# Retrieval in a decoder trunk: 80 sums of key pairs for each head in place of 256

## The chip, the cores and the metric

The kernel runs on one core of a Trainium2 chip. A core has TensorE (PE, matrix products), VectorE (DVE), ScalarE (ACT), GpSimd (POOL) and SyncE (SP, which issues transfers), each with a queue of its own that it works off in order; they wait for one another by semaphores. The metric is the time of one execution on the device in microseconds (us), the median of several runs.

## The reference, cut to what matters

One layer of a decoder trunk is computed for 512 prompt tokens and 64 sample tokens. The part that matters here is the retrieval of single-neuron experts: each token has 8 heads, and each head takes the 16 best of 128 keys on two sides, adds every pair of the two lists, and keeps the 16 best of the 256 sums. From the place of such a sum follow the two keys, and from them the expert's number.

```python
q = (xt @ w_q).astype(jnp.float32).reshape(n, PEER_HEADS, 2, PEER_QDIM // 2)
s = jnp.einsum('nhsd,hskd->nhsk', q, subkeys.astype(jnp.float32))
v_top, i_top = lax.top_k(s, PEER_TOPK)                  # 16 of 128, sorted
cand = (v_top[:, :, 0, :, None] + v_top[:, :, 1, None, :]).reshape(n, PEER_HEADS, PEER_TOPK * PEER_TOPK)
cand_idx = (i_top[:, :, 0, :, None] * PEER_KEYS + i_top[:, :, 1, None, :]).reshape(n, PEER_HEADS, PEER_TOPK * PEER_TOPK)
vals, cpos = lax.top_k(cand, PEER_TOPK)                 # 16 of 256
eidx = jnp.take_along_axis(cand_idx, cpos, axis=-1)
gate = jax.nn.softmax(vals, axis=-1)
```

Both lists are sorted downwards. The sum of entry a of the one and entry b of the other has at least (a + 1)(b + 1) - 1 sums that are no smaller, so it can be among the 16 best only where (a + 1)(b + 1) is at most 16.

## The kernel before

The program is a row of stages: projections, the two mixers, `mix_stage`, then `retrieve_stage`, `gate_matrix_stage`, `experts_stage` and `ple_stage`. Each of these ends with a barrier of all engines. The change touches `retrieve_stage` alone, which lies at 874 to 1182 us of the profiled span.

It does two things side by side. The tokens are taken in five tiles (`TILES`; 128, 128, 128, 64 and 128 rows), with these steps for tile t:

- PE makes the scores of 16 lists of 128 keys (line 1993) and ACT copies them to `scores` (line 1862), one of two buffers.
- DVE runs `select(t)`: for each of the 16 lists the best 8 (`max`, line 1892), their places (`max_index`, 1895), a copy with these 8 struck out (`match_replace`, 1896), the next 8 and their places (1899, 1902). Then for each head the 256 sums of the pairs (line 1909, into the buffer that held the scores), and over these the same five passes (1914 to 1925). Lines 1926 to 1931 subtract the largest value and make two numbers a and b from each place by a shift and a mask. Lines 1936 to 1940 fetch the two keys: a comparison with 0 to 15, a product, a sum, for each side.
- ACT takes exponentials (line 1847); DVE makes the gates (`gates(t)`, lines 1946 to 1952), which stands behind `select(t + 1)` in its queue; PE transposes the picks (line 1982) and ACT copies them to `idxT` (line 1852).

Beside it 50 units of expert products run, for which SP loads a block of weights, ACT makes its high half (line 1831), POOL its low half (line 1879), PE 24 products (line 1571, `dense_products`) and ACT an activation (line 1840). `SELECT_TURNS` says how many units PE does in each tile before and after the transposes of an earlier tile: 4 + 8, 4 + 8, 4 + 4, 4 + 4, 4 + 6. The transposes of tile t stand behind the first four units of tile t + 2, those of the fourth tile behind the last unit; the fifth tile's picks are used as they are. PE's scores of the next tile stand behind all units of the present one. `v.go` sends an instruction without a wait behind it, `v(...)` waits until it is done, `v.wait()` until all are.

The order of each engine is written out by hand; nothing is moved by a scheduler.

Of the kernel before, what the change touches and what calls it, by code (L numbers as in the profile page):

```python
# [15 lines left out]
U32 = mybir.dt.uint32  # L16
# [3 lines left out]
P = 128  # L20
# [28 lines left out]
PH = 8  # L49
# [1721 lines left out]


SELECT_TURNS = ((4, 8), (4, 8), (4, 4), (4, 4), (4, 6))
SELECT_UPS = sum(map(sum, SELECT_TURNS))
SELECT_FROM = [sum(map(sum, SELECT_TURNS[:t])) for t in range(TILES)]
ONE_HOT_UPS = TD // 32
SAMPLE_TILE = TILES - 1
EARLY_GROUPS = (SELECT_UPS + ONE_HOT_UPS) // EG
assert EG * EARLY_GROUPS == SELECT_UPS + ONE_HOT_UPS and SELECT_UPS % 2 == 0


def retrieve_stage(nc, k):

    with ExitStack() as ctx:
        sb = lambda n, s, d=F32: ctx.enter_context(nc.sbuf_tensor(n, s, d))
        sem = k.sem
        sk, iota = sb("subkeys_sb", [P, 16, KEYS]), sb("iota16", [P, 16])
        scores, scr = sb("k_scores", [P, 2, 16, KEYS]), sb("k_scr", [P, 16, KEYS])
        v16, i16, i16f = sb("v16", [P, 16, 16]), sb("i16", [P, 16, 16], U32), sb("i16f", [P, 2, 16, 16])
        eq = sb("eq", [P, PH, 16, 16])  # L1790
        vals, cpos, ab = sb("vals", [P, 2, PH, 16]), sb("cpos", [P, PH, 16], U32), sb("ab", [P, 2, PH, 16], U32)
        abf, idx, gsum = sb("abf", [P, 2, PH, 16]), sb("idx", [P, 2, 3, P]), sb("gsum", [P, 2, PH])
        u_raw, u_hi, u_lo = sb("r_u_raw", [P, EG, KD, P]), sb("r_u_hi", [P, 2, KD, P]), sb("r_u_lo", [P, 2, KD, P])

# [7 lines left out]
        up_done, gelu_done, u_hi_made, u_lo_made = (sem(n) for n in ("r_up", "r_gelu", "r_u_hi_made", "r_u_lo_made"))  # L1802
        N = SELECT_UPS
        block = ctx.enter_context(nc.Block())
# [23 lines left out]
        def _(act):  # L1828
# [4 lines left out]
            def group(first, count):  # L1833
                for n in range(first, first + count):
                    e = n % EG
                    act.wait_ge(up_done, n + 1)
                    if n >= EG and e % 2 == 0:

                        act.wait_ge(k.spilled[e // 2], 16 * (n // EG))
                    nc.scalar.activation(gelu[:, e // 2, e % 2], ps[:, 4 + n % 2, 0:TD], ACT.Gelu_apprx_tanh).then_inc(gelu_done, 1)  # L1840
                    if n + 2 < N:
                        u_high(n + 2)
# [14 lines left out]
            for t in range(TILES):  # L1857
# [4 lines left out]
                nc.scalar.activation(scores[0:m, t % 2].rearrange("p (b n) c -> p b (n c)", b=4), ps[0:m, 0:4, :], ACT.Copy).then_inc(scopied, 1)  # L1862
                half, rest = SELECT_TURNS[t]
                group(SELECT_FROM[t], half)
# [16 lines left out]
        @block.vector  # L1881
        def _(dve):
            v = Chain(dve, vch)
            V = nc.vector

            def select(t):

                m, b = PICK_ROWS[t], t % 2
                sc = scores[0:m, b]
                dve.wait_ge(scopied, t + 1)  # L1890
                for u in range(16):
                    v.go(V.max(v16[0:m, u, 0:8], sc[:, u]))
                v.wait()
                for u in range(16):
                    v.go(V.max_index(i16[0:m, u, 0:8], v16[0:m, u, 0:8], sc[:, u]))
                    v.go(V.match_replace(scr[0:m, u], v16[0:m, u, 0:8], sc[:, u], GONE))
                v.wait()
                for u in range(16):
                    v.go(V.max(v16[0:m, u, 8:16], scr[0:m, u]))
                v.wait()  # L1900
                for u in range(16):
                    v.go(V.max_index(i16[0:m, u, 8:16], v16[0:m, u, 8:16], scr[0:m, u]))
                v.wait()
                v.go(V.tensor_copy(i16f[0:m, b].rearrange("p a b -> p (a b)"), i16[0:m].rearrange("p a b -> p (a b)")))

                cand = sc.rearrange("p a b -> p (a b)").rearrange("p (h c) -> p h c", h=PH)
                left = scr[0:m].rearrange("p a b -> p (a b)").rearrange("p (h c) -> p h c", h=PH)
                for h in range(PH):
                    v.go(V.tensor_tensor(cand[:, h].rearrange("p (a b) -> p a b", a=16),
                                         v16[0:m, 2 * h].unsqueeze(2).to_broadcast([m, 16, 16]),  # L1910
                                         v16[0:m, 2 * h + 1].unsqueeze(1).to_broadcast([m, 16, 16]), ALU.add))
                v.wait()
                for h in range(PH):
                    v.go(V.max(vals[0:m, b, h, 0:8], cand[:, h]))
                v.wait()
                for h in range(PH):
                    v.go(V.max_index(cpos[0:m, h, 0:8], vals[0:m, b, h, 0:8], cand[:, h]))
                    v.go(V.match_replace(left[:, h], vals[0:m, b, h, 0:8], cand[:, h], GONE))
                v.wait()
                V.memset(gsum[0:1, 0, 0:1], 0.0).then_inc(s_used, 1)  # L1920
                for h in range(PH):
                    v.go(V.max(vals[0:m, b, h, 8:16], left[:, h]))
                v.wait()
                for h in range(PH):
                    v.go(V.max_index(cpos[0:m, h, 8:16], vals[0:m, b, h, 8:16], left[:, h]))
                v(V.tensor_copy(gsum[0:m, 0], vals[0:m, b, :, 0]))
                V.tensor_tensor(vals[0:m, b], vals[0:m, b], gsum[0:m, 0].unsqueeze(2).to_broadcast([m, PH, 16]),
                                ALU.subtract).then_inc(eready, 1)
                v.go(V.tensor_scalar(ab[0:m, 0], cpos[0:m], 4, None, ALU.logical_shift_right))
                v(V.tensor_scalar(ab[0:m, 1], cpos[0:m], 15, None, ALU.bitwise_and))  # L1930
                v(V.tensor_copy(abf[0:m].rearrange("p a h c -> p (a h c)"), ab[0:m].rearrange("p a h c -> p (a h c)")))
                if t >= 2:
                    dve.wait_ge(trd, t - 1)
                e3 = eq[0:m].rearrange("p h c a -> p (h c) a")
                for s in range(2):
                    v(V.tensor_tensor(e3, abf[0:m, s].rearrange("p h c -> p (h c)").unsqueeze(2).to_broadcast([m, P, 16]),
                                      iota[0:m].unsqueeze(1).to_broadcast([m, P, 16]), ALU.is_equal))
                    fs = i16f[0:m, b].rearrange("p (h s) a -> p h s a", s=2)[:, :, s]
                    v(V.tensor_tensor(eq[0:m], eq[0:m], fs.unsqueeze(2).to_broadcast([m, PH, 16, 16]), ALU.mult))
                    v(V.tensor_reduce(idx[0:m, b, s], e3, AX.X, ALU.add))  # L1940

            def gates(t):

                m, b = PICK_ROWS[t], t % 2
                dve.wait_ge(ed, t + 1)
                v(V.tensor_reduce(gsum[0:m, 0], vals[0:m, b], AX.X, ALU.add))
                v(V.reciprocal(gsum[0:m, 1], gsum[0:m, 0]))
                if t == SAMPLE_TILE:
                    V.scalar_tensor_tensor(out=k.s_idx[0:m], in0=idx[0:m, b, 0], scalar=float(KEYS), in1=idx[0:m, b, 1],
                                           op0=ALU.mult, op1=ALU.add)  # L1950
                out = k.s_gate[0:m] if t == SAMPLE_TILE else idx[0:m, b, 2]
                V.tensor_tensor(out.rearrange("p (h c) -> p h c", h=PH), vals[0:m, b],
                                gsum[0:m, 1].unsqueeze(2).to_broadcast([m, PH, 16]),
                                ALU.mult).then_inc(tk, 1)

            dve.wait_ge(ld, 32)
            for t in range(TILES):
                select(t)
                if t >= 1:
                    gates(t - 1)  # L1960
            gates(TILES - 1)

        @block.tensor
        def _(pe):
# [21 lines left out]
            for t in range(TILES):  # L1986
# [8 lines left out]
                mm.then_inc(sd, 1)  # L1995
                half, rest = SELECT_TURNS[t]
                group(SELECT_FROM[t], half)
# [10 lines left out]
def gate_matrix_stage(nc, k):  # L2008
# [4 lines left out]
    with ExitStack() as ctx:  # L2013
# [12 lines left out]
        up_done, gelu_done, u_hi_made, u_lo_made = (sem(n) for n in ("gm_up", "gm_gelu", "gm_u_hi_made", "gm_u_lo_made"))  # L2026
        FIRST = SELECT_UPS
        UPS = ONE_HOT_UPS // 2
# [9 lines left out]
        def _(sp):  # L2038
# [25 lines left out]
            for q in range(2):  # L2064
                sp.wait_ge(k.spilled[q], 16 * ((SELECT_UPS // 2 - q + 1) // 2))
            for b in range(2):
# [898 lines left out]
```

## Time and profile before

| | us |
|---|---|
| median of 3 runs | 2481.58 (2476.61 to 2482.66) |
| profiled execution | 2492.35 |
| its span, first to last instruction | 2490.7 |
| PE busy in the span | 2196.4 (88%) |
| DVE busy | 1747.6 (70%) |
| ACT busy | 771.1 (31%) |
| POOL busy | 721.2 (29%) |

The shares are means over stages with different limits. What a change inside a stage is worth is read from that stage: which engine waits for which there, and which wait ends last. Times in the rows further down are us from the span's start unless they are marked ns. In the views by time a row gives the start, the length, the engine, line, operation, output <- input, shapes and count, and in brackets how long the engine was idle in front of it and who ended that.

### The profile page before, as it was taken

What the parts mean: (1) busy time and instruction counts of PE and PEld (TensorE: products, weight loads), DVE (VectorE), ACT (ScalarE), POOL (GpSimd) and SP (SyncE); (2) the same over time, 40 slices, a digit from 0 to 9 for tenths busy, and PEclk for the clock granted to TensorE, in tenths of its full rate; (3) what the DMA queues carried; (4) which work ended last, traced back from release to release, by engine and by line L of the source; (5) the groups of instructions that cost most, each with busy time, mean ns of one, the idle gap of its engine ahead of it and who ended that gap; (6) DMA issues with size and microseconds to landing.
All of it is one profiled execution on the core that took longest, in us unless ns stands there. A gap on an engine that the chain in (4) does not pass through costs nothing. (4 is left out here: it accounts for less than half of the span.)

```text
span 2490.7 us, 36671 instructions
## 1 busy us (share of the span) xinstructions
PE 2196.4 (88%) x11589; PEld 1911.2 (77%) x11589; DVE 1747.6 (70%) x3908; ACT 771.1 (31%) x1376; POOL 721.2 (29%) x653
## 2 busy tenths in 40 slices
PE   7885599777698999985899689999999999999979
PEld 5444389544488989974888678888899999999968
DVE  6845300466322089999999689999889898888852
ACT  2021211354322233331454323333323233232331
POOL 0411311201132344441444222222433333333302
PEclk9987799588898999997999899999999999999999
DMA  5204623412421144440766667778888787878721
GB/s 207 19 24 61 206 81 122 122 56 89 153 77 52 50 172 145 133 146 25 256 186 204 201 246 291 291 291 308 305 286 294 274 309 273 303 274 286 254 89 39
DMA packets 194121, 448.24 MB, mean 180 GB/s; under 512 B 26401, under 2 KB 109602, under 8 KB 184610
## 3 DMA queue, kind: packets, MB, share of 16 engines
q1 hardware_dynamic: 140082, 222.74, 27.3%
q0 software_dynamic: 44288, 156.92, 18.8%
q10 hardware_dynamic: 9648, 67.24, 6.8%
q8 instruction: 60, 0.98, 0.2%
q14 instruction: 43, 0.35, 0.0%
HBM read 394.07 MB, written 54.80 MB: 180 GB/s over the span
## 5 line engine op out<-in xcount | busy, mean ns | idle before, releaser
L2591 PE MATMUL e_ps<-w_hi,v_hi 128*128 128x448 f32 x1024 | 379.8, 371 | 25.2 <-DVE w_lo L2485 15.3
L2591 PE MATMUL e_ps<-w_lo,v_hi 128*128 128x448 f32 x1024 | 378.3, 369 | 0.0
L2591 PE MATMUL e_ps<-w_hi,v_lo 128*128 128x448 f32 x1024 | 378.1, 369 | 0.0
L2591 PEld LDWEIGHTS e_ps<-w_hi,v_hi 128*128 128x128 f32 x1024 | 194.1, 190 | 48.9 <-issue 23.5
L2591 PEld LDWEIGHTS e_ps<-w_hi,v_lo 128*128 128x128 f32 x1024 | 194.1, 190 | 18.0
L2591 PEld LDWEIGHTS e_ps<-w_lo,v_hi 128*128 128x128 f32 x1024 | 194.1, 190 | 17.7
L1571 PE MATMUL e_ps<-x_hi,u_hi 128*128 128x448 f32 x512 | 189.5, 370 | 17.9 <-DVE u_lo L2420 17.9
L1571 PE MATMUL e_ps<-x_lo,u_hi 128*128 128x448 f32 x512 | 189.4, 370 | 0.0
L1571 PE MATMUL e_ps<-x_hi,u_lo 128*128 128x448 f32 x512 | 189.2, 370 | 0.0
L2430 DVE TENSOR_TENSOR hT<-hT,e_ps 128x448 f32<-128x448 f32 x256 | 157.5, 615 | 31.6 <-PE e_ps L2591 31.6
L2324 ACT ACTIVATE v_hi<-v_raw 128x512 fp32r<-128x512 f32 x256 | 157.2, 622 | 68.0 <-PE e_ps L2591 62.3
L2424 DVE TENSOR_TENSOR v_lo<-v_raw,v_hi 128x512 fp32r<-128x512 f32 x256 | 174.9, 685 | 0.3
L1879 POOL TENSOR_TENSOR r_u_lo<-r_u_raw,r_u_hi 128x1024 fp32r<-128x1024 f32 x50 | 125.0, 2500 | 167.4 <-ACT r_u_hi L1831 167.4
L2276 POOL DMA_INDIRECT s_rows<-in_v_rows,s_idx x62 | 76.2, 1229 | 296.3 <-DVE s_rows L2451 295.7
L2125 PE MATMUL g_ps<-one_hot 128*128 128x128 f32 x896 | 134.1, 289 | 22.6 <-DVE one_hot L2093 22.6
L2125 PEld LDWEIGHTS g_ps<-one_hot 128*128 128x128 f32 x896 | 126.1, 194 | 32.8 <-DVE one_hot L2093 29.8
L1571 PE MATMUL r_ps<-x_hi,r_u_hi 128*128 128x448 f32 x400 | 148.2, 371 | 1.0 <-POOL r_u_lo L1879 1.0
L1571 PE MATMUL r_ps<-x_hi,r_u_lo 128*128 128x448 f32 x400 | 147.0, 368 | 0.0
L1571 PE MATMUL r_ps<-x_lo,r_u_hi 128*128 128x448 f32 x400 | 147.0, 368 | 0.0
L2093 DVE TENSOR_SCALAR one_hot<-iota,idx_T 128x128 f32<-128x128 f32 x448 | 144.0, 341 | 0.0
L2335 ACT ACTIVATE w_hi<-w_raw 128x448 fp32r<-128x448 f32 x128 | 73.6, 575 | 219.7 <-DVE w_raw L2494 200.6
L2353 ACT ACTIVATE e_act<-e_ps 128x448 f32<-128x448 f32 x64 | 34.8, 545 | 326.7 <-PE e_ps L1571 326.7
(538 smaller groups left out, 5059.5 us busy)
## 6 DMA issues: line engine op xcount, KB each, us to landing
v_raw<-in_v_tab ACTq DMA_DIRECT2D x62, 1024.0 KB, 7.0
u_raw<-in_u_tab SPq DMA_DIRECT2D x64, 512.0 KB, 6.0
gate_scr<-gate_stage SPq DMA_DIRECT2D x14, 2048.0 KB, 9.3
mixT<-gate_scr SPq DMA_DIRECT2D x32, 896.0 KB, 5.9
r_u_raw<-in_u_tab SPq DMA_DIRECT2D x50, 512.0 KB, 3.9
gelu_scr<-mixT SPq DMA_DIRECT2D x32, 448.0 KB, 2.7
acts_and_rows<-gelu_scr SPq DMA_DIRECT2D x16, 896.0 KB, 7.3
m_w_raw<-in_w_mix SPq DMA_DIRECT2D x24, 512.0 KB, 3.5
```

The source lines that it names most:

```text
L1571: mm = pe.matmul(out, as_r(u), as_r(x[:, i, 0:TD]), start=(i == 0 and n == 0), stop=(i == KD - 1 and n == 2))
L1879: nc.gpsimd.tensor_tensor(as_r(u_lo[:, n % 2]), u_raw[:, n % EG], u_hi[:, n % 2], ALU.subtract).then_inc(u_lo_made, 1)
L2093: nc.vector.tensor_scalar(oh2[:, n % 8], iota[:], k.idxT[:, 1, at], k.idxT[:, 2, at], ALU.is_equal, ALU.mult).then_inc(hot, 1)
L2125: mm = nc.tensor.matmul(ps[:, q % 4, KEYS * (n % 4):KEYS * (n % 4) + KEYS], oh1[:, n % 8], oh2[:, n % 8], start=True, stop=True)
L2276: pool.indirect_dma_start(out=ring[j], out_offset=None, in_=k.d[table], in_offset=bass.IndirectOffsetOnAxis(ap=s_idx[:, slot:slot + 1], ax ...
L2324: nc.scalar.activation(as_r(v_hi[:, c % 4]), v_raw[:, c // 4, c % 4], ACT.Copy).then_inc(v_hi_made, 1)
L2335: nc.scalar.activation(as_r(w_hi[:, b, e]), w_raw[:, e % 2], ACT.Copy).then_inc(w_hi_made, 1)
L2353: nc.scalar.activation(act_[:, e % 2], ps[:, e % 2, 0:TD], ACT.Gelu_apprx_tanh).then_inc(gelu_done, 1)
L2424: nc.vector.tensor_tensor(as_r(v_lo[:, c % 4]), v_raw[:, c // 4, c % 4], v_hi[:, c % 4], ALU.subtract).then_inc(v_lo_made, 1)
L2430: nc.vector.tensor_tensor(h, h, ps[:, 4 + c % 4, 0:TD], ALU.add).then_inc(added, 1)
L2591: mm = nc.tensor.matmul(ps[:, 4 + c % 4, 0:TD], as_r(v[:, c % 4, e]), as_r(w[:, b, e]), start=(e == 0 and n == 0), stop=(e == EG - 1 and n ...
```

## The change

A head's candidates are 80 sums and not 256. `CAND_ROWS` lists four blocks of them, each with its place in the 80, its first row a, its number of rows and its width: rows 0 and 1 with 16 entries of the second list, rows 2 and 3 with 8, rows 4 to 7 with 4, rows 8 to 15 with 2. Each block is one instruction for all 8 heads. The passes over the candidates are written as before, on arrays of 80. Since a place in the 80 no longer splits into a and b by one shift and one mask, seven integer instructions take the place of two; two of these shift by an amount that is itself a tensor (`level`).

```diff
+CAND = 80
+CAND_ROWS = ((0, 0, 2, 16), (32, 2, 2, 8), (48, 4, 4, 4), (64, 8, 8, 2))
...
+        ab2 = sb("ab_parts", [P, 2, PH, 16], U32)
...
-                cand = sc.rearrange("p a b -> p (a b)").rearrange("p (h c) -> p h c", h=PH)
-                left = scr[0:m].rearrange("p a b -> p (a b)").rearrange("p (h c) -> p h c", h=PH)
-                for h in range(PH):
-                    v.go(V.tensor_tensor(cand[:, h].rearrange("p (a b) -> p a b", a=16),
-                                         v16[0:m, 2 * h].unsqueeze(2).to_broadcast([m, 16, 16]),
-                                         v16[0:m, 2 * h + 1].unsqueeze(1).to_broadcast([m, 16, 16]), ALU.add))
+                cand, left = (a.rearrange("p a b -> p (a b)")[:, 0:CAND * PH].rearrange("p (h c) -> p h c", h=PH) for a in (sc, scr[0:m]))
+                pair = v16[0:m].rearrange("p (h s) a -> p h s a", s=2)
+                for at, row, n, width in CAND_ROWS:
+                    v.go(V.tensor_tensor(cand[:, :, at:at + n * width].rearrange("p h (a b) -> p h a b", a=n),
+                                         pair[:, :, 0, row:row + n].unsqueeze(3).to_broadcast([m, PH, n, width]),
+                                         pair[:, :, 1, 0:width].unsqueeze(2).to_broadcast([m, PH, n, width]), ALU.add))
...
-                v.go(V.tensor_scalar(ab[0:m, 0], cpos[0:m], 4, None, ALU.logical_shift_right))
-                v(V.tensor_scalar(ab[0:m, 1], cpos[0:m], 15, None, ALU.bitwise_and))
+                level, place = ab2[0:m, 0], ab2[0:m, 1]
+                v.go(V.tensor_scalar(level, cpos[0:m], 4, None, ALU.logical_shift_right))
+                v(V.tensor_scalar(place, cpos[0:m], 15, 16, ALU.bitwise_and, ALU.bitwise_or))
+                v(V.tensor_tensor(place, place, level, ALU.logical_shift_left))
+                v.go(V.tensor_scalar(ab[0:m, 0], place, 5, None, ALU.logical_shift_right))
+                v(V.tensor_scalar(place, place, 31, None, ALU.bitwise_and))
+                v(V.tensor_tensor(place, place, level, ALU.logical_shift_right))
+                v(V.tensor_scalar(ab[0:m, 1], place, 15, None, ALU.bitwise_and))
```

On DVE, in the first tile, from the cast of the keys' places to the first passes over the candidates, before (`i16f` holds the keys' numbers, `k_scores` the candidates, `vals` the best 8, `cpos` their places, `k_scr` what is left):

```order
L1904 CAST i16f<-i 128x256
L1909 TENSOR_TENSOR k_scores<-v 128x256 x8
L1914 MAX vals<-k_scores 128x8 x8
L1917 MAX_INDEX cpos<-vals,k_scores 128x8
L1918 MATCH_REPLACE k_scr<-vals,k_scores 128x256
```

and with the change:

```order
L1908 CAST i16f<-i 128x256
L1913 TENSOR_TENSOR k_scores<-v 128x8x32
L1913 TENSOR_TENSOR k_scores<-v 128x8x16 x3
L1918 MAX vals<-k_scores 128x8 x8
L1921 MAX_INDEX cpos<-vals,k_scores 128x8
L1922 MATCH_REPLACE k_scr<-vals,k_scores 128x80
```

Eight sums of 256 columns have become one of 256 and three of 128, and what is struck out is 80 wide; the passes keep their number and their order.

On DVE, in the first tile, from the last pass to the fetching of the keys, before (`gsum` is the largest value, `ab` and `abf` the numbers a and b, `eq` the comparison):

```order
L1925 MAX_INDEX cpos<-vals,k_scr 128x8 x8
L1926 COPY gsum<-vals 128x8
L1927 TENSOR_TENSOR vals<-vals,gsum 128x128
L1929 TENSOR_SCALAR ab<-cpos 128x128
L1930 TENSOR_SCALAR ab<-cpos 128x128
L1931 CAST abf<-ab 128x256
L1936 TENSOR_TENSOR eq<-abf,iota 128x2048
```

and with the change (`ab_parts` holds `level` and `place`):

```order
L1929 MAX_INDEX cpos<-vals,k_scr 128x8 x8
L1930 COPY gsum<-vals 128x8
L1931 TENSOR_TENSOR vals<-vals,gsum 128x128
L1934 TENSOR_SCALAR ab_parts<-cpos 128x128
L1935 TENSOR_SCALAR ab_parts<-cpos 128x128
L1936 TENSOR_TENSOR ab_parts<-ab_parts 128x128
L1937 TENSOR_SCALAR ab<-ab_parts 128x128
L1938 TENSOR_SCALAR ab_parts<-ab_parts 128x128
L1939 TENSOR_TENSOR ab_parts<-ab_parts 128x128
L1940 TENSOR_SCALAR ab<-ab_parts 128x128
L1941 CAST abf<-ab 128x256
L1946 TENSOR_TENSOR eq<-abf,iota 128x2048
```

Five instructions more stand between the subtraction and the comparison; nothing changes its place.

## Rows read from the trace of the kernel before

**Rows 1.** Windows, second and fourth tile: stretch, length, busy us (count), clock, DMA.

```profile
945.00:1007.00 62.00, 62.00 (x320) 57.22 (x319) 60.61 (x216) 22.26 (x29) 29.80 (x12) 1.00 0.44 146
1066.00:1125.00 59.00, 46.93 (x248) 43.14 (x246) 58.34 (x216) 20.15 (x25) 24.24 (x10) 0.92 0.42 137
```

**Rows 2.** Waits in 860 to 1220: us in total, times, longest.

```profile
DVE v L1892 <- ACT k_scores L1862: 118.1, 3, 115.1
PE r_ps L1982 <- DVE idx L1952: 35.3, 2, 23.2
```

**Rows 3.** DVE in order of time, where its tiles begin and end.

```profile
1007.66 3.19 DVE L1892 MAX8 v<-k_scores 128x8 f32<-128x128 f32 x16 [1.05 <-ACT k_scores L1862]
...
1065.33 0.29 DVE L1952 TENSOR_TENSOR idx<-vals,gsum 128x128 f32<-128x128 f32 x1
...
1124.65 0.29 DVE L1952 TENSOR_TENSOR idx<-vals,gsum 128x128 f32<-128x128 f32 x1
...
1180.81 0.29 DVE L1952 TENSOR_TENSOR mixT<-vals,gsum 128x128 f32<-128x128 f32 x1
```

**Rows 4.** PE in order of time, its transposes of the third and fourth tiles.

```profile
1125.00 0.90 PE L1982 MATMUL r_ps<-ident,idx 128*128 128x128 f32 x3 [12.07 <-DVE idx L1952]
...
1180.18 0.58 PE L1982 MATMUL r_ps<-ident,idx 64*128 64x64 f32 x3 [23.23 <-DVE idx L1952]
```

**Rows 5.** DVE in order of time, first tile.

```profile
882.92 3.19 DVE L1892 MAX8 v<-k_scores 128x8 f32<-128x128 f32 x16 [115.07 <-ACT k_scores L1862]
...
902.16 2.48 DVE L1904 CAST i16f<-i 128x256 f32<-128x256 uint32 x1
904.57 2.76 DVE L1909 TENSOR_TENSOR k_scores<-v 128x256 f32<-128x256 f32 x8
907.36 2.71 DVE L1914 MAX8 vals<-k_scores 128x8 f32<-128x256 f32 x8
...
922.47 1.64 DVE L1926 COPY gsum<-vals 128x8 f32<-128x8 f32 x1
924.14 0.29 DVE L1927 TENSOR_TENSOR vals<-vals,gsum 128x128 f32<-128x128 f32 x1
924.35 0.22 DVE L1929 TENSOR_SCALAR ab<-cpos 128x128 uint32<-128x128 uint32 x1
924.49 0.22 DVE L1930 TENSOR_SCALAR ab<-cpos 128x128 uint32<-128x128 uint32 x1
924.74 0.29 DVE L1931 CAST abf<-ab 128x256 f32<-128x256 uint32 x1
925.07 2.29 DVE L1936 TENSOR_TENSOR eq<-abf,iota 128x2048 f32<-128x2048 f32 x1
927.40 4.38 DVE L1939 TENSOR_TENSOR eq<-eq,i16f 128x2048 f32<-128x2048 f32 x1
```

**Rows 6.** Groups of DVE by shape: count, busy us, mean ns, idle before.

```profile
L1914 DVE MAX8 vals<-k_scores 128x8 f32<-128x256 f32 x32 | 10.9, 412 | 0.1
...
L1420 DVE MAX8 sa_top<-sa_score 128x8 f32<-128x33 f32 x8 | 1.0, 182 | 0.1
```

**Rows 7.** POOL in order of time.

```profile
921.67 2.40 POOL L1879 TENSOR_TENSOR r_u_lo<-r_u_raw,r_u_hi 128x1024 fp32r<-128x1024 f32 x1 [2.48 <-ACT r_u_hi L1831]
926.58 3.05 POOL L1879 TENSOR_TENSOR r_u_lo<-r_u_raw,r_u_hi 128x1024 fp32r<-128x1024 f32 x1 [2.50 <-ACT r_u_hi L1831]
...
1060.44 4.23 POOL L1879 TENSOR_TENSOR r_u_lo<-r_u_raw,r_u_hi 128x1024 fp32r<-128x1024 f32 x1 [2.50 <-ACT r_u_hi L1831]
```

**Rows 8.** DVE in order of time, third tile, beside the last of these.

```profile
1060.13 2.29 DVE L1939 TENSOR_TENSOR eq<-eq,i16f 128x2048 f32<-128x2048 f32 x1
```

**Rows 9.** ACT in order of time, its reading of three units in a row.

```profile
1058.87 0.55 ACT L1840 ACTIVATE mixT<-r_ps 128x448 f32<-128x448 f32 x1 [3.41 <-PE r_ps L1571]
...
1063.77 0.54 ACT L1840 ACTIVATE mixT<-r_ps 128x448 f32<-128x448 f32 x1 [3.40 <-PE r_ps L1571]
...
1069.91 0.54 ACT L1840 ACTIVATE mixT<-r_ps 128x448 f32<-128x448 f32 x1 [4.65 <-PE r_ps L1571]
```

## The prediction

> **What bounds the kernel now.** I read the page first (88% of the span has a busy TensorE, PE), then the waits of the retrieval stage, then the order of its five tiles of tokens. A change to VectorE (DVE) work pays only where something waits for DVE, so the stage is read tile by tile.
>
> In the second tile PE is busy for 62.00 of 62 us [rows 1]: twelve units of expert products and the next tile's scores fill it without a gap. DVE is the one that waits there, for the scores that ScalarE (ACT) copies out after PE's twelfth unit; its three such waits are the 115.1 us before its first work of the stage and two short ones [rows 2], of which one is 1.05 us, at 1007.66 [rows 3]. Tiles 0 and 1 are therefore paced by PE, and what DVE saves in them becomes a longer wait.
>
> From 1007.66 on it is the other way round. DVE goes on without a gap: the third tile's work, with the gates of the second, ends at 1065.33 + 0.29; the fourth with the gates of the third at 1124.65 + 0.29; the last ends at 1180.81 + 0.29 = 1181.10 [rows 3]. PE waits for it twice, 12.07 us before the transposes of the third tile's picks and 23.23 us before those of the fourth [rows 4], the 35.3 us of [rows 2]; in 1066 to 1125 PE is busy for only 46.93 of 59 us and DVE for 58.34 [rows 1]. So **the stage ends when DVE has done three tiles in a row from 1007.66 on**, and a saving of S per tile is worth 3 S, not 5 S.
>
> **The change part by part.** All its edits are on DVE in `select`, five times (rows of order in the section on the change).
>
> *Passes over the candidates.* Per head there are five: two MAX8, two FIND_INDEX8, one MATCH_REPLACE8. The 40 passes of 256 columns run from 907.36 to 922.47, 15.11 us, or 1.889 us per head. The same five passes over 128 columns (for 16 lists) run from 882.92 to 902.16, 19.24 us, or 1.202 us per list [rows 5]. The slope is 0.687 / 128 = 5.36 ns per column for five passes, so at 80 columns one head costs 1.202 - 48 x 0.00536 = 0.945 us and eight cost 7.56: **7.55 us less**. A width below 80 bears out the straight line: MAX8 lasts 182 ns at 33 columns and 412 at 256 [rows 6], 1.03 ns per column, against 5.36 / 5 = 1.07.
>
> *Sums.* Eight of 128x256 take 904.57 to 907.36, 2.79 us, 0.35 each. Now there are four for all heads together, one of 256 columns and three of 128; a sum of 128 columns holds the queue for 924.14 to 924.35, 0.21 us [rows 5]. 0.35 + 3 x 0.21 = 0.98: **1.81 less**. Their innermost runs are 16, 8, 4 and 2 long, which the trace doesn't show; if each cost as much as a 256-column one it would be 1.40, and 1.39 less.
>
> *Finding the places.* Before: two shift/mask operations and the cast, 924.35 to 925.07, 0.72 us [rows 5]. Now five TENSOR_SCALARs, two TENSOR_TENSOR shifts and the cast, nearly all waiting for the one in front. From the same rows: without a wait a TENSOR_SCALAR takes 0.14, with one 0.25, a 128-column TENSOR_TENSOR with a wait 0.32, the cast 0.33. 0.14 + 0.25 + 0.32 + 0.14 + 0.25 + 0.32 + 0.25 + 0.33 = 2.00: **1.28 more**. A shift whose amount is a second tensor of integers is in no row. I take the float sum's price, since the shape is the same and the integer TENSOR_SCALARs (0.22) show no penalty for integers; the ends are 0.25 each (1.14 more in all) and two passes each (0.6 more, 1.9 in all). The new tensor of 128 integers twice per partition costs no time.
>
> So S = 7.55 + 1.81 - 1.28 = **8.1 us per tile** (7.0 to 8.3), and three tiles give 24.2 (21 to 25).
>
> *What the move does to GpSimd (POOL) and back to PE.* POOL makes a low half of expert weights for each of PE's units, about 2.4 us in every 4.9, and some DVE instructions and POOL's exclude each other. The copy of 8 columns at 922.47 lasts 1.64 us, until 924.11, and POOL's operation that started at 921.67 ends at 924.07. The cast at 902.16 lasts 2.48 against 0.29 for the one at 924.74 [rows 5]. In the other direction POOL's operation of 1060.44 takes 4.23 [rows 7], since the product that DVE began at 1060.13 runs to 1062.42 [rows 8]: it is 4.23 - 2.40 = 1.83 us late, and PE's unit after it ends late: ACT's reading of it comes 6.14 us after the last one instead of 4.90 [rows 9], 1.24 us lost. So PE forgives about 0.6 us.
>
> The Trainium skill (SBUF — State Buffer, Who interferes with whom) says that a VectorE instruction with two SBUF inputs contends with a GpSimd instruction that reads SBUF, that the shared ports are locked for a whole instruction, and that issue order decides who blocks. The rows above agree with it in both directions; by it alone the two new shifts would be able to wait for POOL too, up to once for each POOL operation.
>
> Now the copy's wait ties the chain behind it to POOL's end. Before, the first comparison (925.07 to 927.36) overlapped POOL's next start, 926.58, which then lasted 3.05 us [rows 5, 7]: 0.65 late, just about forgiven. With 1.28 us more in front, the comparison starts at 926.35, 0.23 us ahead of POOL, and ends at 928.64; POOL is 2.06 late, PE 2.06 - 0.6 = 1.45 late. (Should the chain be over 0.23 us longer, the comparison waits for POOL, and the product behind it delays POOL's next operation instead: about the same price.) My reckoning of the earlier part of the tile puts the copy at about 913.2, inside POOL's operation of that time too, so I take this for once in each of tiles 0 and 1, where PE is the pace: **2.9 us lost** (0 to 6). In tiles 2 to 4 such a delay costs PE alone: it would reach the transposes of the third tile's picks at 1125.00 - 12.07 + 2.9 + about 1.7 = 1117.5, after DVE has delivered them (1124.94 - 16.2 + 2.9 = 1111.6), and be done with its six last units of 4.9 us at about 1147.5. DVE ends at 1181.10 - 24.2 + 2.9 = 1159.8. The 12.07 us wait is gone, PE still waits about 12 us at the end, and DVE is still what ends the stage.
>
> *DVE's own waits for POOL* in tiles 2 to 4: each tile has some three before (1.4 for the copy, 2.2 for the cast, 4.38 - 2.29 = 2.1 for a product [rows 5]), and as many are to be expected behind the same instructions now. Net 0, and up to 4 us either way.
>
> What follows the stage starts behind a barrier and moves as a whole; in front of it PE has waited for many us before, and does so after.
>
> Sum: 24.2 - 2.9 = 21.3 us. The profiled execution would go from 2492.35 (span 2490.7) to 2471; it stands 10.8 us above the median of the three runs, all of it outside this reckoning, so the median goes from 2481.58 to **2460.3**.
>
> **The rivals.**
> - *Collisions eat more.* PE loses up to 6 us in tiles 0 and 1 and DVE waits 4 us more: 21 to 24 less 10, a gain of 11 to 16, 2466 to 2471. For it: the rows show waits of 1.5 to 2.2 us at each collision, and the chain is tied to POOL's end. Against it: a POOL operation can be met only once, and 2.5 us lie free behind each.
> - *No collisions lost*: PE keeps its pace, DVE's waits shrink: 24 to 29, 2453 to 2457.
> - *The rest gives it back*, or the shorter lists pay little (a fixed cost per pass that the line doesn't show): within 7 us of before, about 2477. For it: the three runs alone lie 6 us apart; against it: rows at 33, 128 and 256 columns lie on one line, and the width of 80 is in the order of the changed kernel.
> - *Slower: the two shifts by a tensor of amounts are slow.* Their place is the same chain of three tiles. They begin to decide where the chain costs 8 us more per tile than I gave it, 4 us more for each shift, some fourteen times the row of 0.29; at 5.5 us more each the stage is 3 x 11 - 21.3 = 11.7 us longer, 2493. Nothing in the trace speaks for it.
>
> **How the numbers follow.** Forecast (gain 16 to 24): 0.70. More collisions: 0.14. None lost: 0.07. Given back or little paid: 0.07. Slow shifts: 0.02. The range takes in the forecast, the second case and most of the third, 2453 to 2470. A measurement of this kernel can tell about 0.3%, 7.4 us: faster than 2474.1 is all of the first three, 0.91; same 0.07; slower 0.02.
>
> **What would show each step.** MAX8 at 80 columns near 0.23 us, passes of a tile near 7.6 us in a row, sums near 1.0, integer operations near 2.0 from shift to comparison. DVE waits near 10 us for scores in front of tiles 1 and 2; none behind. PE's wait in front of the third tile's transposes is gone, the one in front of the fourth's is near 12 us. POOL operations of over 4 us, one or two in each tile, with a unit of 6.3 us behind them. I am wrong if tiles 2 to 4 don't shorten by 7 to 9 us each, or if the time from 1007 to the stage's end shortens and the rest grows.

## The result and the profile after

| | before | after |
|---|---|---|
| median of 9 runs, us | 2482.66 (2476.61 to 2495.82) | 2459.01 (2454.79 to 2475.19) |
| ratio, 95% interval | | 0.9905 (0.9881 to 0.9929) |
| profiled execution's span, us | 2490.7 | 2456.4 |
| DVE's part of the retrieval stage, first MAX8 to last gate, us | 298.18 | 274.67 |
| of it tiles 0 and 1 | 124.74 | 127.32 |
| of it tiles 2 to 4 | 173.44 | 147.35 |

Faster by 23.65 us by the medians; 21.3 were forecast (2460.3, range 2453 to 2470). One execution of this study's last kernel (even units and three buffers) took 4418.14 us and is left out of that kernel's numbers. The stage's length is read from DVE in order of time: from the first MAX8 over scores, 882.92 before [rows 5] and 883.92 after, to the end of the last gate, 1180.81 + 0.29 [rows 3] and 1158.31 + 0.28. Below, tile t is counted from its first MAX8 to that of the next.

DVE of the kernel after, in order of time, where tiles 0, 1, 2 and 4 begin and where the gates of tiles 1, 2 and 4 end; these answer to [rows 3]:

```profile
883.92 3.19 DVE L1896 MAX8 v<-k_scores 128x8 f32<-128x128 f32 x16 [115.17 <-ACT k_scores L1866]
...
947.62 3.19 DVE L1896 MAX8 v<-k_scores 128x8 f32<-128x128 f32 x16 [11.81 <-ACT k_scores L1866]
...
1011.24 3.19 DVE L1896 MAX8 v<-k_scores 128x8 f32<-128x128 f32 x16 [10.86 <-ACT k_scores L1866]
...
1061.86 0.29 DVE L1962 TENSOR_TENSOR idx<-vals,gsum 128x128 f32<-128x128 f32 x1
...
1111.94 0.29 DVE L1962 TENSOR_TENSOR idx<-vals,gsum 128x128 f32<-128x128 f32 x1
1112.15 3.19 DVE L1896 MAX8 v<-k_scores 128x8 f32<-128x128 f32 x16
...
1158.31 0.28 DVE L1962 TENSOR_TENSOR mixT<-vals,gsum 128x128 f32<-128x128 f32 x1
```

What DVE saved in tiles 0 and 1 has become waiting for scores, 11.81 and 10.86 us, and behind 1011.24 it waits for no scores. The waits of DVE and PE, the answer to [rows 2] and [rows 4] (us in total, times, longest; then PE in order of time):

```profile
DVE v L1896 <- ACT k_scores L1866: 137.8, 3, 115.2
PE r_ps L1992 <- DVE idx L1962: 11.5, 1, 11.5
```

```profile
1157.69 0.58 PE L1992 MATMUL r_ps<-ident,idx 64*128 64x64 f32 x3 [11.50 <-DVE idx L1962]
```

The 12.07 us in front of the third tile's transposes are gone, the 23.23 in front of the fourth's are 11.50.

The profiled spans differ by 34.3 us, 11 more than the stages. The surplus lies elsewhere: from the last product of the gate matrix to the last of the experts (first and last start of these groups, by tile) it was 2396.7 - 1392.5 = 1004.2 us before and 994.0 after:

```profile
L2125 PE MATMUL g_ps<-one_hot x896: 270/275/582, 1188.1 to 1392.5; 128*128 128x128 f32 x180
L2618 PE MATMUL e_ps<-ident,s_sum x8: 272/272/273, 2396.0 to 2396.7; 128*128 128x128 f32 x8
```

```profile
L2135 PE MATMUL g_ps<-one_hot x896: 270/275/582, 1165.7 to 1370.0; 128*128 128x128 f32 x180
L2628 PE MATMUL e_ps<-ident,s_sum x8: 270/272/273, 2363.3 to 2364.0; 128*128 128x128 f32 x8
```

That stretch, which no edit here touches, lay between 990.6 and 1005.1 us over the eleven profiled executions of this study, and a kernel with the change in its last three tiles had the longest. I take it for scatter (the nine runs of the kernel before alone lie 19.2 us apart), and it is the reason why the experiments are read by the length of the retrieval stage first and by the total second.

### The profile page after: what moved, and what is told of

It is laid out like the page before. It is cut to its first block and busy times, and to the rows that moved or that the text cites. A ratio compares the mean times of both kernels' runs of the same rounds, so it can differ in the third digit from the quotient of the medians.

```text
span 2456.4 us, 36676 instructions
## 1 busy us (share of the span) xinstructions
PE 2184.2 (89%) x11589; PEld 1909.7 (78%) x11589; DVE 1701.9 (69%) x3913; ACT 770.3 (31%) x1376; POOL 732.7 (30%) x653
## 5 line engine op out<-in xcount | busy, mean ns | idle before, releaser
L1883 POOL TENSOR_TENSOR r_u_lo<-r_u_raw,r_u_hi 128x1024 fp32r<-128x1024 f32 x50 | 134.2, 2685 | 146.3 <-ACT r_u_hi L1835 146.3
```

The costliest lines, as they stand in the source:

```text
L1883: nc.gpsimd.tensor_tensor(as_r(u_lo[:, n % 2]), u_raw[:, n % EG], u_hi[:, n % 2], ALU.subtract).then_inc(u_lo_made, 1)
```

## The experiments

### Where the shorter passes pay: the last three tiles, or the first two

In the kernel after, the two changed places of `select` are put under a condition on the tile; the other branch holds the lines of the kernel before. For the second kernel the condition is `t in (0, 1)`.

```diff
-                cand, left = (a.rearrange("p a b -> p (a b)")[:, 0:CAND * PH].rearrange("p (h c) -> p h c", h=PH) for a in (sc, scr[0:m]))
+                if t in (2, 3, 4):
+                    cand, left = (a.rearrange("p a b -> p (a b)")[:, 0:CAND * PH].rearrange("p (h c) -> p h c", h=PH) for a in (sc, scr[0:m]))
...
+                else:
+                    cand = sc.rearrange("p a b -> p (a b)").rearrange("p (h c) -> p h c", h=PH)
...
```

Expected of the kernel with the 80 sums in tiles 2 to 4:

> The 80 sums in the third, fourth and fifth tile alone; the first two tiles keep the 256 sums and their two integer instructions. Stage length is from DVE's first MAX8 over scores to its last gate: 298.2 us in the kernel before, 274.7 in the changed one. Theory (the first two tiles are paced by PE, the new chain there only costs PE 1.3 us each through POOL, and three tiles in a row on DVE set the end): tiles 0 and 1 take 124.7 us as before, tiles 2 to 4 about 147.3, stage 272 (270 to 274), 2.6 shorter than the changed kernel; no POOL operation of over 4 us in the first two tiles. Rival (each tile's saving counts alike): 298.2 - 3 x 4.7 = 284.

and of the one with them in tiles 0 and 1:

> The 80 sums in the first two tiles alone. Theory: DVE gets done some 9 us earlier in each and waits for scores; PE loses 1.3 us in each through POOL; stage 298.2 + 2.6 = 300.8 (300 to 302), so no faster than the kernel before, 2 to 3 us slower. Rival (each tile's saving counts alike): 298.2 - 2 x 4.7 = 288.8.

Measured, for the stage and in brackets for tiles 0 and 1 + tiles 2 to 4: 272.03 us (124.71 + 147.32) and 300.91 us (127.28 + 173.63). DVE of the first and of the second, in order of time, the beginning of tile 2 (views that end at 1010 us, so with 14 and 6 of the 16 MAX8) and the end:

```profile
1007.41 2.81 DVE L1896 MAX8 v<-k_scores 128x8 f32<-128x128 f32 x14 [1.04 <-ACT k_scores L1866]
...
1154.45 0.28 DVE L1974 TENSOR_TENSOR mixT<-vals,gsum 128x128 f32<-128x128 f32 x1
```

```profile
1008.97 1.26 DVE L1896 MAX8 v<-k_scores 128x8 f32<-128x128 f32 x6 [10.85 <-ACT k_scores L1866]
...
1182.31 0.29 DVE L1974 TENSOR_TENSOR mixT<-vals,gsum 128x128 f32<-128x128 f32 x1
```

In the totals: 0.9908 (0.9888 to 0.9928) and 1.0025 (1.0006 to 1.0045) of the kernel before. Both stages lie where the theory had them. All of the gain comes from three tiles; in the first two the same edit shortens DVE's work and lengthens the kernel. The rivals' 284 and 288.8 are out.

### Why PE loses time in the first two tiles: the chain alone

The kernel before with five more integer instructions whose result isn't used, two of them on two tensors (a mask and a shift):

```diff
+        ab2 = sb("ab_parts", [P, 2, PH, 16], U32)
...
                 v(V.tensor_scalar(ab[0:m, 1], cpos[0:m], 15, None, ALU.bitwise_and))
+                spare = ab2[0:m, 0], ab2[0:m, 1]
+                v(V.tensor_tensor(spare[1], cpos[0:m], cpos[0:m], ALU.bitwise_and))
+                v.go(V.tensor_scalar(spare[0], cpos[0:m], 5, None, ALU.logical_shift_right))
+                v(V.tensor_scalar(spare[1], spare[1], 31, None, ALU.bitwise_and))
+                v(V.tensor_tensor(spare[1], spare[1], spare[0], ALU.logical_shift_right))
+                v(V.tensor_scalar(spare[1], spare[1], 15, None, ALU.bitwise_and))
```

> The kernel before with five further integer instructions, two of them TENSOR_TENSORs, behind the two that it has; their result isn't used. Theory: 1.3 us more per tile on DVE; in tiles 0 and 1 DVE has 2.0 and 1.05 us to spare, but the comparison now starts ahead of POOL, which is 2 us late and PE 1.3 to 1.5 in each; tiles 2 to 4 are 3.9 longer; stage 298.2 + 2.7 + 3.9 = 304.8 (303 to 307), POOL operations of over 4 us in tiles 0 and 1. Rival (the chain costs only its own length): 298.2 + 3.9 = 302.1 and no such POOL operation there.

Measured: 301.61 us, 127.27 in tiles 0 and 1 and 174.34 in tiles 2 to 4; total 1.0026 (0.9997 to 1.0055). DVE, POOL and ACT of this kernel in order of time, first tile:

```profile
923.57 2.29 DVE L1943 TENSOR_TENSOR eq<-abf,iota 128x2048 f32<-128x2048 f32 x1
```

```profile
923.76 4.33 POOL L1880 TENSOR_TENSOR r_u_lo<-r_u_raw,r_u_hi 128x1024 fp32r<-128x1024 f32 x1 [2.50 <-ACT r_u_hi L1832]
```

```profile
927.09 0.54 ACT L1841 ACTIVATE mixT<-r_ps 128x448 f32<-128x448 f32 x1 [3.40 <-PE r_ps L1571]
933.34 0.55 ACT L1841 ACTIVATE mixT<-r_ps 128x448 f32<-128x448 f32 x1 [4.76 <-PE r_ps L1571]
```

The comparison starts 0.19 us ahead of POOL, POOL takes 4.33 instead of 2.40, and the unit after it 6.25 us instead of 4.90: what the kernel after does, made in the kernel before by the chain alone. That half of the expectation held (2.5 us lost in the first two tiles). The other half didn't: tiles 2 to 4 grew by 0.9 us, not by 3.9, so that the stage lies below the 303 to 307 us that I expected, next to the rival's 302.1, although the POOL operations that the rival ruled out are there.

The lengths of the tiles tell how much of this is work and how much waits. The beginning and the cast of the last tile, DVE in order of time, in the kernel before and in this one:

```profile
1124.86 3.18 DVE L1892 MAX8 v<-k_scores 128x8 f32<-128x128 f32 x16
...
1144.09 2.33 DVE L1904 CAST i16f<-i 128x256 f32<-128x256 uint32 x1
```

```profile
1124.60 3.18 DVE L1893 MAX8 v<-k_scores 128x8 f32<-128x128 f32 x16
...
1143.84 1.94 DVE L1905 CAST i16f<-i 128x256 f32<-128x256 uint32 x1
```

The last tile of the kernel before is 56.24 us long, of which its cast waits 2.04 for POOL (2.33 in place of 0.29): 54.20 of work. In this kernel it is 57.13 with a wait of 1.65: 55.48, so 1.28 more, as expected. Taking 55.48 us for the last tile, and 1.04 less for a tile that makes one set of gates and not two (1.80 us for the two, 0.76 for one), the three tiles hold 164.4 us of work, and 174.34 - 164.4 = 10.0 us are waits for POOL. In the kernel before it is 173.44 - 160.5 = 12.9. The longer chain brought 3.9 us of work and met POOL 2.9 us less.

### The same chain taken out of the kernel after

```diff
-                level, place = ab2[0:m, 0], ab2[0:m, 1]
-                v.go(V.tensor_scalar(level, cpos[0:m], 4, None, ALU.logical_shift_right))
...
-                v(V.tensor_scalar(ab[0:m, 1], place, 15, None, ALU.bitwise_and))
+                v.go(V.tensor_scalar(ab[0:m, 0], cpos[0:m], 4, None, ALU.logical_shift_right))
+                v(V.tensor_scalar(ab[0:m, 1], cpos[0:m], 15, None, ALU.bitwise_and))
```

> The changed kernel with the two integer instructions of the kernel before in place of the seven; the places in the list of 80 are then split into a and b in a way that doesn't belong to them, so other experts are picked. Theory (the longer chain is what makes the first comparison meet POOL): tiles 0 and 1 lose the two units of 6.3 us on PE, 124.7 in place of 127.3 us; tiles 2 to 4 are 3 x 1.3 shorter; stage 274.7 - 2.6 - 3.9 = 268.2 (266 to 270). Rival (it is the earlier end of the passes that meets POOL, whatever the chain): POOL operations of over 4 us stay in tiles 0 and 1, stage 274.7 - 3.9 = 270.8 or more.

Measured: 271.53 us, 126.27 + 145.26. The stage is longer than the theory's 266 to 270 and lies where the rival had it; tiles 0 and 1 lie between the two. The first tile behaves as the theory says: the first comparison starts early enough, POOL is only 0.64 late, and the tile is 62.39 long as before. The second is 63.88 long, and its loss has another place, the product for the second key. POOL and DVE of this kernel in order of time, first tile, then second:

```profile
928.38 2.41 POOL L1883 TENSOR_TENSOR r_u_lo<-r_u_raw,r_u_hi 128x1024 fp32r<-128x1024 f32 x1 [2.40 <-ACT r_u_hi L1835]
...
990.78 4.53 POOL L1883 TENSOR_TENSOR r_u_lo<-r_u_raw,r_u_hi 128x1024 fp32r<-128x1024 f32 x1 [2.41 <-ACT r_u_hi L1835]
```

```profile
928.39 4.55 DVE L1943 TENSOR_TENSOR eq<-eq,i16f 128x2048 f32<-128x2048 f32 x1
...
990.79 2.29 DVE L1943 TENSOR_TENSOR eq<-eq,i16f 128x2048 f32<-128x2048 f32 x1
```

Both times the two begin within 0.01 us of each other, POOL first by the record. In the first tile POOL goes ahead and DVE's product takes 4.55; in the second DVE goes ahead and POOL takes 4.53. Which of the two is decided by less than the trace resolves. In tiles 2 to 4 the work is 1.32 less per tile (a last tile of 45.50 with a wait of 0.38, against 46.44 without one), and the waits for POOL are 12.0 in place of 10.1 us. So the chain does make the first comparison meet POOL, and without it something else may. The rival is half right too: what counts is when DVE's long instructions begin beside POOL's (their phase), and the chain is one thing that moves it.

### One unit further ahead

If PE loses time only since POOL may be just one unit ahead of it, a third buffer must give it back.

```diff
-        u_raw, u_hi, u_lo = sb("r_u_raw", [P, EG, KD, P]), sb("r_u_hi", [P, 2, KD, P]), sb("r_u_lo", [P, 2, KD, P])
+        u_raw, u_hi, u_lo = sb("r_u_raw", [P, EG, KD, P]), sb("r_u_hi", [P, 3, KD, P]), sb("r_u_lo", [P, 3, KD, P])
...
-                    if n + 2 < N:
-                        u_high(n + 2)
+                    if n + 3 < N:
+                        u_high(n + 3)
...
-                if n >= 2:
-                    pool.wait_ge(up_done, n - 1)
+                if n >= 3:
+                    pool.wait_ge(up_done, n - 2)
...
```

> The changed kernel with three buffers in place of two for the high and the low halves of the expert weights, so that ACT and POOL may be one unit further ahead of PE. Theory (PE loses 1.3 to 1.5 us where POOL is 2 us late only because it is at most one unit ahead): POOL operations of about 4.3 us stay, units of 6.3 us are gone, tiles 0 and 1 take 124.7 us in place of 127.3; what DVE waits for POOL in the last three tiles is dealt out anew (10.1 us now, 10 to 13 in the kernels so far), stage 272 (269 to 275). Rival (PE loses the time for another reason, its own order or ACT): the first two tiles stay at 127.3.

Measured: 274.10 us, 124.56 in tiles 0 and 1. POOL and ACT of this kernel in order of time, first tile:

```profile
918.17 4.37 POOL L1883 TENSOR_TENSOR r_u_lo<-r_u_raw,r_u_hi 128x1024 fp32r<-128x1024 f32 x1 [2.49 <-ACT r_u_hi L1835]
923.07 3.90 POOL L1883 TENSOR_TENSOR r_u_lo<-r_u_raw,r_u_hi 128x1024 fp32r<-128x1024 f32 x1 [0.53 <-ACT r_u_hi L1835]
```

```profile
921.50 0.55 ACT L1844 ACTIVATE mixT<-r_ps 128x448 f32<-128x448 f32 x1 [3.40 <-PE r_ps L1571]
926.40 0.55 ACT L1844 ACTIVATE mixT<-r_ps 128x448 f32<-128x448 f32 x1 [3.41 <-PE r_ps L1571]
```

POOL is as late as before and the units stay at 4.90 us. The edit lets ACT run further ahead as well as POOL; that it was POOL's lateness which PE felt is told by this wait of the kernel after, which is gone here:

```profile
PE r_ps L1571 <- POOL r_u_lo L1883: 3.2, 3, 1.1
```

But the stage is shorter by only 0.6: the last tile is 48.63 us in place of 46.44, a wait of 2.2 us in its sums (DVE in order of time; 1.02 is what they take without a wait):

```profile
1129.22 3.25 DVE L1913 TENSOR_TENSOR k_scores<-v 128x256 f32<-128x256 f32 x4
```

Total 0.9891 (0.9862 to 0.9920), not to be told from the kernel after.

### The units dealt out evenly

The first two tiles have DVE waiting for PE, the last ones PE waiting for DVE. With ten units in each tile PE needs about 53 us, and DVE took 46 to 51 in the last three tiles of the kernel after.

```diff
-SELECT_TURNS = ((4, 8), (4, 8), (4, 4), (4, 4), (4, 6))
+SELECT_TURNS = ((4, 6), (4, 6), (4, 6), (4, 6), (4, 6))
```

In the kernel after:

> The changed kernel with ten units of PE in each tile (4 + 6) in place of 12, 12, 8, 8, 10. Theory (DVE now needs 46 to 50 us a tile, PE 10 x 4.9 + 3.6 = 52.6, so PE never waits inside the stage and both end together): the third tile starts 2 x 9.8 us earlier, the stage is PE's 50 units, about 265 to 268 us, 7 to 10 shorter than the changed kernel's 274.7; PE's wait in front of the last transposes falls from 11.5 us to under 3. Rival (DVE and POOL collide in every tile and PE, now the pace everywhere, loses 2.6 or more in each): 270 to 274, and the total is the same as that of the changed kernel.

and once more beside the kernel with three buffers as well:

> The changed kernel with ten units of PE in each tile once more, beside the one with three buffers: stage 268 as before, total 2451 (2447 to 2456), 8 us below the changed kernel's 2459.

> Ten units of PE in each tile and three buffers for the halves. Theory: with ten units a tile PE lost about 1.1 us behind each of five late POOL operations, 5.4 us; with three buffers none of it, stage 268.3 - 5.4 = 263 (261 to 266), total some 5 us below that of the kernel with ten units alone. Rival (DVE's waits for POOL grow and DVE becomes the pace): 267 or more, PE waiting over 4 us in front of the last transposes.

Measured: 268.25 and 268.28 us with the even units, 262.79 with three buffers too. Waits in the stage with the even units (us in total, times, longest), and with both:

```profile
DVE v L1896 <- ACT k_scores L1866: 120.8, 5, 115.2
PE r_ps L1571 <- POOL r_u_lo L1883: 5.4, 5, 1.1
...
PE r_ps L1992 <- DVE idx L1962: 2.3, 1, 2.3
```

```profile
DVE v L1896 <- ACT k_scores L1866: 116.0, 2, 115.2
PE r_ps L1992 <- DVE idx L1962: 3.6, 1, 3.6
```

With the even units alone PE is the pace, as the theory has it: DVE waits for scores in front of every tile. But the theory had no loss behind POOL, and PE loses 1.1 us behind a late POOL operation five times, 5.4 us; the stage is 6.4 us shorter than that of the kernel after, where 7 to 10 were expected. The third buffer gives the loss back (5.5 us). DVE then waits for scores only once more after its first (0.8 us, in front of tile 1) and PE for DVE at the end: from tile 1 on DVE is the pace, as the rival had it, though the stage is shorter than the rival's 267.

What a further gain would have to take away are DVE's waits for POOL. Reckoned as above, the work of tiles 2 to 4 is 3 x 46.44 - 2.08 = 137.2 us with the change. With the even units these tiles take 160.6 us, of which 2.5 are waits for scores: 20.8 are waits for POOL, and with three buffers 157.75 - 137.2 = 20.5, twice the 10.1 of the kernel after.

The totals were 0.9883 (0.9862 to 0.9904) and 0.9885 (0.9862 to 0.9909) of the kernel before with the even units, medians 2450.76 and 2454.57; with three buffers 0.9886 (0.9859 to 0.9913), median 2456.73, so the further 5 us that I expected in the total don't show there. These are the shortest retrieval stages of the study, 6 and 12 us below the kernel after; in the totals the scatter of the experts' stretch is as large, and the intervals overlap with the kernel after's. That a version beats the kernel after is shown for the stage, not for the total.

Is it the even units alone that pay? The kernel before with them:

> The kernel before (256 sums) with ten units of PE in each tile. Theory: DVE needs 56 to 60 us a tile against PE's 52.6, so DVE sets the pace from the second tile on: its five tiles in a row, 59.4 + 59.4 + 57.9 + 59.3 + 56.2 = 292 us, give a stage of 291 to 294 in place of 298.2, 4 to 7 us less. Rival (the order of the units alone brings what it brings the changed kernel, whatever DVE's length): 298.2 - 8 = 290 or less, with PE's wait in front of the last transposes gone.

Measured: 285.46 us, total 0.9955 (0.9935 to 0.9976), 12.7 us less. That is more than the theory's 4 to 7 and fits the rival's number (290 or less), but not its mechanism, since PE's last wait is still there (row of PE in order of time), and DVE waits for scores only before its first tile (times and us as above):

```profile
1167.49 0.58 PE L1982 MATMUL r_ps<-ident,idx 64*128 64x64 f32 x3 [23.22 <-DVE idx L1952]
```

```profile
DVE v L1892 <- ACT k_scores L1862: 115.1, 1, 115.1
```

DVE in order of time, where its first and third tiles begin and the last one ends:

```profile
882.93 3.19 DVE L1892 MAX8 v<-k_scores 128x8 f32<-128x128 f32 x16 [115.07 <-ACT k_scores L1862]
...
1001.97 3.19 DVE L1892 MAX8 v<-k_scores 128x8 f32<-128x128 f32 x16
...
1168.11 0.28 DVE L1952 TENSOR_TENSOR mixT<-vals,gsum 128x128 f32<-128x128 f32 x1
```

DVE is the pace, as the theory said. The last three tiles are 166.42 long in place of 173.44, though they hold the same work: 5.9 us of waits for POOL and not 12.9. My sum had carried the tiles over with their waits. The first two give the other 5.7 us (119.04 for 124.74).

## Why the prediction was right, point by point

*The bound.* Three tiles, not five: held, and shown by the two kernels with the change in some tiles only.

*The work per tile.* Forecast 8.1 us, measured 54.20 - 46.44 = 7.76. DVE of the kernel after, first tile, in order of time, which answers to [rows 5]:

```profile
905.56 1.02 DVE L1913 TENSOR_TENSOR k_scores<-v 128x256 f32<-128x256 f32 x4
906.61 1.25 DVE L1918 MAX8 vals<-k_scores 128x8 f32<-128x80 f32 x8
...
914.39 0.93 DVE L1930 COPY gsum<-vals 128x8 f32<-128x8 f32 x1
...
915.56 0.22 DVE L1934 TENSOR_SCALAR ab_parts<-cpos 128x128 uint32<-128x128 uint32 x1
...
917.59 2.29 DVE L1946 TENSOR_TENSOR eq<-abf,iota 128x2048 f32<-128x2048 f32 x1
919.92 4.35 DVE L1949 TENSOR_TENSOR eq<-eq,i16f 128x2048 f32<-128x2048 f32 x1
```

The passes take 906.61 to 914.39, 7.78 us (forecast 7.56), the sums 1.05 (0.98), the integers 917.59 - 915.56 = 2.03 (2.00). The groups by shape (count, busy us, mean ns, idle before), which answer to [rows 6], show the two terms that were taken from neighbours:

```profile
L1918 DVE MAX8 vals<-k_scores 128x8 f32<-128x80 f32 x32 | 5.0, 229 | 0.1
...
L1936 DVE TENSOR_TENSOR ab_parts<-ab_parts 128x128 uint32<-128x128 uint32 x4 | 1.2, 292 | 0.1
```

229 ns lie on the line between 182 at 33 columns and 412 at 256, and a shift by a tensor of integers costs what a float sum does, 0.29.

*PE's loss in tiles 0 and 1.* Forecast 2.9, measured 127.32 - 124.74 = 2.6. POOL of the kernel after in order of time, first tile, which answers to [rows 7]:

```profile
917.77 4.35 POOL L1883 TENSOR_TENSOR r_u_lo<-r_u_raw,r_u_hi 128x1024 fp32r<-128x1024 f32 x1 [2.48 <-ACT r_u_hi L1835]
922.67 3.88 POOL L1883 TENSOR_TENSOR r_u_lo<-r_u_raw,r_u_hi 128x1024 fp32r<-128x1024 f32 x1 [0.55 <-ACT r_u_hi L1835]
```

The comparison begins at 917.59, 0.18 us ahead of the first of these (0.23 were worked out), and POOL is 1.95 late (2.06).

*DVE's waits for POOL in tiles 2 to 4.* Set at nought, up to 4 us either way; 12.9 before, 10.1 after, a gain of 2.8. This is the mis-sized term, though inside its stated bound, and with 7.76 in place of 8.1 it makes up the difference: 3 x 7.76 + 2.8 - 2.6 = 23.5 for the stage, where 24.2 - 2.9 = 21.3 stood. I had no way to size it: with the 256 sums the runs show it at 5.9 to 13.1 us, with the 80 sums at 10.1 to 20.8. How many operations POOL has beside these tiles doesn't order them (25 in the kernel before, 27 in the one with even units and the least waits). I put the differences down to the phase; no run moves the phase alone, so that this is argued and not shown.

*What follows the stage* moved as a whole, as far as the scatter lets one say: the medians differ by 23.65 us, the stages by 23.51. That the median lies within 1.3 us of the forecast is in part luck: its interval is some 6 us wide on either side, and the waits, 2.8 us better than set, made up for about 1 us less saved in the work.

*The signs.* One of them came out against me by its letter: tiles 2 to 4 were each to shorten by 7 to 9 us, and they shortened by 7.05, 9.24 and 9.80. It was badly set, since a tile's length holds its waits for POOL: these changed by +0.7, -1.5 and -2.0 us, and what is left is the 7.76 of work each time. The POOL operations of over 4 us came once in each of the first three tiles, twice in the fourth and not at all in the fifth.

*The rivals.* Slow shifts: out, 292 ns. Given back by the rest: out within the scatter. No collisions lost: right in that DVE's waits shrank, wrong in that PE lost its 2.6 us. More collisions: the fear was right in kind, and the kernel with the added chain shows the PE half of it, but in tiles 2 to 4 they came out smaller. (Its gain, 21 to 24 less 10, is 11 to 14 us and not 11 to 16.)

*The rows behind the exclusion.* The copy and the cast that the prediction shows waiting for POOL read one tensor each, so they say nothing of the rule on two inputs that the prediction quotes. The product at 927.40 does, which took 4.38 us behind POOL's operation of 926.58, and so does the one at 1060.13, behind which POOL took 4.23.

## What to carry to other kernels

Before an engine's work is shortened, mark tile by tile who waits for whom, and once it is shorter deal the other engine's work out anew: here the same edit was worth 26 us in three tiles and minus 2.6 in the other two. Where two engines exclude each other, an edit also moves the phase between them, worth several us in either direction; one more buffer took the loss from the third engine behind them (PE), but not the waits of the two for each other. Read such an edit by work (length less waits) and by waits apart.

## What the runs showed of the hardware that I had not expected

The order of two claims decides which engine waits, and it is settled more finely than the trace shows: POOL 2.41 and DVE 4.55 us in one tile, POOL 4.53 and DVE 2.29 in the next, of the same kernel, with POOL's start recorded 0.01 us ahead both times. The Trainium skill (SBUF — State Buffer, Who interferes with whom) says that issue order decides who blocks, not the shape of the operations. These rows agree as to the shape, which is the same in both; the order they can't show. All eleven profiles together can: in the stage's rows a copy, a cast or a product of DVE and a POOL operation begin within 0.03 us of each other 32 times. Where POOL's start is recorded 0.02 or 0.03 us ahead, POOL went ahead 10 times of 10; at 0.01 it did 11 times of 13; where both have the same time, DVE went ahead 8 times of 9. So it isn't a toss, but a reckoning that is good to 0.1 us can't foresee it.

And the waits that follow are not fixed by DVE's instructions: 5.9 us and 12.9 us in three tiles with the same instructions, only dealt out otherwise around them.
